# The first two weight tiles of each normalised stage side by side, the second three chunks behind, in a two-layer hybrid decoder trunk

## The reference

```python
for i in range(DEPTH):                       # DEPTH = 2
    hn = rms_norm(h, norm_mix_pre[i])
    mix = even_mixer(hn, ...) if i % 2 == 0 else odd_mixer(hn, ...)
    h = h + rms_norm(mix, norm_mix_post[i])
    hn = rms_norm(h, norm_mlp_pre[i])
    m = jnp.square(jax.nn.relu(hn @ w_mlp_up[i])) @ w_mlp_down[i]
    h = h + rms_norm(m, norm_mlp_post[i])
    gate = jax.nn.sigmoid(rms_norm(h, ple_norm[i]) @ w_ple_gate[i])
    h = h + gate * (p[i] @ w_ple_proj[i])
```

## Time and profile before

| | |
|---|---|
| median of 3 runs | 2984.29 us (2972.61 to 2984.62) |
| the profiled execution | 2986.78 us, its span 2985.0 us |
| PE busy | 2857.4 us (96%) |
| DVE, ACT, POOL busy | 1139.9 (38%), 830.6 (28%), 923.3 us (31%) |
| mean clock granted to TensorE | 0.98 of full |
| idle time of PE that ended with DVE's `XL` (L2116) | 27.4 us, 15 times |

### The profile page before, as it was taken

The page is one execution under the profiler, slowest core; times in us unless marked ns, Lnnn a source line. Parts: engine busy times, 40 slices in busy tenths (PEclk is TensorE's granted clock), DMA queues, the critical chain, the costliest instruction groups (busy, mean ns, idle before and its releaser), DMA issues.

```text
span 2985.0 us, 36478 instructions
## 1 busy us (share of the span) xinstructions
PE 2857.4 (96%) x13804; PEld 2328.6 (78%) x13804; DVE 1139.9 (38%) x1837; ACT 830.6 (28%) x1455; POOL 923.3 (31%) x610
## 2 busy tenths in 40 slices
PE   8998999989999999999999999888899999999998
PEld 4896888868888888886788777777588888888867
DVE  3425877243222222225432444675522221222254
ACT  3304777241110000114311222575501110000250
POOL 2321156323332333333221223213333332333422
PEclk9999999999999999999998999699999999999999
DMA  4456632201111111111242313554011111111112
GB/s 156 139 183 225 164 93 72 98 29 50 43 49 49 49 49 46 45 64 36 85 173 75 38 44 38 122 118 134 29 50 45 47 49 49 49 48 44 64 36 78
DMA packets 105220, 227.79 MB, mean 76 GB/s; under 512 B 41379, under 2 KB 53155, under 8 KB 104791
## 3 DMA queue, kind: packets, MB, share of 16 engines
q1 hardware_dynamic: 93224, 181.91, 22.1%
q10 hardware_dynamic: 11872, 44.21, 3.8%
HBM read 188.36 MB, written 41.39 MB: 77 GB/s over the span
## 4 chain that ended last, share of the span: by engine, by line
PE 85%; DVE 8%; issue 3%; ACT 3%; DMA 1%; SPq 0%; POOL 0%; ACTq 0%; DVEq 0%; POOLq 0%
PE ACC L1304 65%; PE ACC L1601 5%; PE OP L1570 3%; PE TR L1537 3%; PE ACC L1523 3%; PE OP L1413 2%; PE ACC L1394 2%; DVE XL L2116 1%; DVE H L2136 1%; DVE T L2133 1%; DVE PB L2326 1%; ACT PB L1909 1%; ACT PT L1902 1%; DVE PT L2347 1%; PE ACC L1496 1%
## 5 line engine op out<-in xcount | busy, mean ns | idle before, releaser
L1110 POOL CAST WH<-RAW 128x1024 fp32r<-128x1024 f32 x188 | 197.9, 1052 | 1442.3 <-PE ACC L1304 1390.5
L1304 PE MATMUL ACC<-XH,WH 128*128 128x512 f32 x1728 | 553.4, 402 | 33.9 <-DVE XL L2116 27.4
L1304 PE MATMUL ACC<-XL,WH 128*128 128x512 f32 x1728 | 536.0, 392 | 0.0
L1304 PE MATMUL ACC<-XH,WL 128*128 128x512 f32 x1728 | 535.5, 391 | 0.0
L1112 POOL TENSOR_TENSOR WL<-RAW,WH 128x1024 fp32r<-128x1024 f32 x188 | 453.1, 2410 | 21.6
L1304 PEld LDWEIGHTS ACC<-XH,WH 128*128 128x128 f32 x1728 | 324.7, 189 | 130.4 <-issue 50.6
L1855 ACT ACTIVATE HH<-T 128x1024 fp32r<-128x1024 f32 x64 | 67.9, 1062 | 1149.7 <-DVE T L2158 1149.7
L1304 PEld LDWEIGHTS ACC<-XH,WL 128*128 128x128 f32 x1728 | 326.3, 189 | 68.6
L1304 PEld LDWEIGHTS ACC<-XL,WH 128*128 128x128 f32 x1728 | 326.3, 189 | 68.4
L2165 DVE TENSOR_TENSOR M<-M,ACC 128x1024 f32<-128x1024 f32 x128 | 156.3, 1221 | 481.8 <-PE ACC L1304 479.6
L1304 PE MATMUL ACC<-HH,WH 128*128 128x512 f32 x1024 | 317.0, 391 | 3.3 <-DVE M L2165 3.1
(11 more groups left out here) (251 smaller groups left out, 3501.9 us busy)
## 6 DMA issues: line engine op xcount, KB each, us to landing
RAW<-in_w SPq DMA_DIRECT2D x203, 512.0 KB, 3.5
QK<-y_odds SPq DMA_DIRECT2D x56, 256.0 KB, 5.8
QK<-y_foxs SPq DMA_DIRECT2D x48, 256.0 KB, 5.8
y_foxs<-HALVES ACTq DMA_DIRECT2D x8, 1024.0 KB, 5.0
y_foxv<-HALVES ACTq DMA_DIRECT2D x4, 1024.0 KB, 4.5
BIAS<-y_f SPq DMA_DIRECT2D x8, 512.0 KB, 7.6
H<-in_xT ACTq DMA_DIRECT2D x8, 512.0 KB, 6.5
y_h<-H ACTq DMA_DIRECT2D x8, 512.0 KB, 2.7
```

The costliest lines, as they stand in the source:

```text
L1110: nc.gpsimd.tensor_copy(WH[:, slot], RAW[:, slot]).then_inc(s_whi, 1)
L1304: mm = nc.tensor.matmul(acc[:, h * HALF:(h + 1) * HALF], w(k), x[:, k, h * HALF:(h + 1) * HALF], start=first and k == k0 and w is ws and x ...
```

## The change

In the five stages `x`, `h0`, `g0`, `h1`, `g1` (not `x1`) PE works on the first two tiles in turns: once the product of chunk k of the first tile is issued and k is 3 or more, it issues chunk k - 3 of the second tile; after the first tile's last chunk (and the `stats` of chunk 7 that its hook issues) follow chunks 4, one after another to 7, of the second. The second tile is of the next unit, in the other weight slot and the other half of `ACC`. Its waits (weights split, half evacuated) move with it: they stand before its chunk 0. Its place in the old order is left out.

```diff
+BEHIND = 3
+BESIDE = ("x", "h0", "g0", "h1", "g1")
...
-            def weights(name, ready=None, after=None):
+            def weights(name, ready=None, after=None, beside=False):
                 seg = segs[name]
+                def second(k):
+                    u = seg.iters[0][1]
+                    t, slot = u.tiles[0], u.no % 2
+                    xh, xl = operands(u.src)
+                    if k == 0:
+                        pe.wait_ge(s_split, u.no + 1)
+                        evacuated([t], 0)
+                    mm = three_pass(ACC[:, t.pair], k, k + 1, lambda _: WH[:, slot, k * P:(k + 1) * P],
+                                    lambda _: WL[:, slot, k * P:(k + 1) * P], xh, xl, k == 0, k == DC - 1)
+                    if k == DC - 1:
+                        mm.then_inc(s_tile, 1)
+                        if after:
+                            after(t)
...
+                        if beside and pos == 1:
+                            continue
...
                             for m in range(len(u.tiles)):
                                 for k in order:
                                     product(m, k)
+                                    if beside and pos == 0 and k >= BEHIND:
+                                        second(k - BEHIND)
+                            for k in range(DC - BEHIND, DC) if beside and pos == 0 else ():
+                                second(k)
...
-                return dict(ready=ready, after=after)
+                return dict(ready=ready, after=after, beside=name in BESIDE)
```

## The result

| | before | changed |
|---|---|---|
| median, 20 runs each | 2973.5 us (2969.44 to 2988.86) | 2989.5 us (2975.3 to 2995.17) |
| changed / before | | 1.0034 (95% interval 1.0020 to 1.0049) |
| profiled execution | 2986.78 us, span 2985.0 | 2990.04 us, span 2988.2 |
| PE, DVE, ACT, POOL busy | 2857.4, 1139.9, 830.6, 923.3 us | 2856.1, 1145.9, 830.9, 925.5 us |
| idle of PE that ended with `XL` | 27.4 us, 15 times | 24.1 us, 3 times |

The ratio is about 10 us slower (6 to 15), within the 0.5% that was forecast as no measurable change and not nothing. The medians are 16 us apart, which says more than it should: the run times of either kernel lie in two groups some 13 us apart.

A forecast was written before the change was run, and what follows sets the result against it. PE's own work was taken as the bound (85% of the span). Terms -1.71 - 1.69 - 1.66 + 3.64 + 1.9 + 1.5 = +2.0 us on the profiled 2986.78, less 2.49 for the median: 2986.3 us, range 2973 to 2991.

The forecast's parts named there:

- The verdict: Whole kernel: no measurable change, less than 0.5% or 15 us; chances faster 0.04, same 0.92, slower 0.04.
- its own case: Whole kernel: gains and losses nearly cancel at +2.0 us, giving 2986.3 us, within 2981 to 2989; chance 0.66.
- The gains: PE's waits for the DVE's chunks vanish: -1.71 us in h0, -1.69 in h1, -1.66 each in g1 and g0.
- (a): Third tile in h0, h1, g1: the first tile's half of `ACC` is freed in time, 0.45 us over; priced at 0.
- (b): Fourth tile in x: PE waits for cq 1's evacuation behind the angle instructions, +1.5 us; lower bound 0.
- (c): g0: x1's first `stats` wait 5.2 us for a square that is 3.79 us later; +3.64 us net.
- (d): g0, behind the wait for x1's statistic: PE's clock drops to its lower level, +1.9 us, bounds 0 and 2.8.
- Only the gains count: Whole kernel: no late-statistic wait in g0 and x's angles shrink, so -6.7 us, 2977.6 us; chance 0.08.
- The change does nothing: All five stages: PE keeps the DVE's pace and the late statistics are hidden, 2984.3 us; chance 0.06.
- The rival of the spread: Whole kernel: the changed kernel falls more often to the short run's time, median 2974.6 us; chance 0.17.
- The low clock that lasts: Layer 1's attention: more stretches at the half clock level, each up to 19 us, 3005.3 us; chance 0.03.

## Why the prediction was right or wrong

**The verdict** (no measurable change, below 0.5%) was right by the ratio of 1.0034, and 2989.5 us lies in 2973 to 2991, above the 2981 to 2989 of its own case. Part of that is luck: two of the three runs of the kernel before that were shown lay in its upper group, so the base of 2984.29 was 11 us above the median of 20 runs. Against that median the forecast of +2.0 us stands beside a measured +16, or +10 by the ratio. The working should have given +5.4 by its own way of counting, and +7.1 with what h0 and h1 really gained in that trace. What is left up to +10 is mostly the larger share of long runs (14 of 20 for 9 of 20, some 13 us each, or 3 us).

**The gains** of 1.71, 1.69 and 1.66 us came as 1.60, 1.59 and 1.53, counted from chunk 3 as the prediction did, and in x nothing was there to gain. That the short waits go, and that turns between two tiles cost PE nothing, held to 0.1 us. What the sum missed is that the wait it took from the trace is not a fixed price: in h0 and h1 it is what the DVE is slower than PE, and shrinks by what PE itself has lost up to chunk 3. In the changed trace PE had lost 0.8 us to the clock, and of 1.60 and 1.59 us only 0.79 and 0.67 were gained.

**(a) The third tile's slack** of 0.45 us held in all the stages; no row shows a wait there.

**(b) The fourth tile in x** was priced at 1.50 us and waits 1.49. The lower bound of 0 (the slow instruction on the angles might not fall beside POOL's split) did not come: it fell on another of the ten.

**(c) The late statistic in g0** was named as the step that decides, and it did. The shift was 3.79 us and the wait 5.2 by the prediction; 7.8 was measured. The mis-sized term is the path from `R` to the square, which was moved as a block. POOL's split is tied to the end of the second tile, which came 5.4 us earlier against the first tile's evacuation (7.49 us behind it before, 2.06 now), and ran over two of the path's instructions; that POOL issues what it issued, in the same order, was right, but not beside whom. With the split held back the wait is the 5.21 us predicted. (a) and (b) asked what waits for the moved work, and (c) what is late; nothing asked what is now early. So its price was +3.64 and is +6.42.

**(d) The clock behind the wait** was priced at 1.9 us, and is 2.0. That a break brings the lower level is less sure than the prediction has it: behind the 2.90 us break in `ple0` on which it rests, the changed trace has the full level (0.70 us for the 1.19 before).

**The rivals.** "Only the gains count" is out: the wait is there. "The change does nothing" is out. The rival of the spread had the right fact, two groups of runs, and the wrong place: it named the stretch around 1900 to 1950, where the clock of the lower execution is as low as the upper one's (0.61 over the 50 us from 1884, for 0.62). The groups come from the block of small products at 1578 to 1604. It also had the sign wrong: the changed kernel has more of the long runs, not fewer, and that is most of what lies between the change's own price and 10 us. The low clock that lasts was half right in that, but a group of runs is 13 us apart and no more than that is added.

## What to carry to other kernels

When work is pulled forward on an in-order engine, list three things: what now comes later behind it (each statistic, evacuation and release, with the engines that wait for it), what now ends earlier (and which other engine it sets off beside whom), and which waits the new work really lies in. A short wait behind a slower engine is worth only what is left of it in the execution at hand. Here 0.7 to 1.6 us a stage was won and 8.4 us lost by one statistic of the *next* stage that stood in the same queue; issuing it one tile later took the loss away for nothing. Where run times come in two groups, settle the groups first: compare group with group, or find and remove what splits them, before a difference of a few us is read.

## What the runs showed of the hardware

TensorE's granted clock fell to the lower level in a stretch in which PE was busy all the time, with 64-column products between 128 x 128 weight loads (0.53 granted over 25.2 us), and in another kernel's trace with the same block it didn't (1.00 over 14.3 us). The same products taken in eights between dense 512-column ones no longer split the run times. Behind the same idle time of 2.90 us the first pair of matmuls took 1.19 us in one execution and 0.70 in another. And a DVE sum of two operands took 3.25 us for 1.23 beside a POOL subtraction, which took 3.20 for 2.40 itself.
